# Start of a decoder layer on TensorE: inputs and the first three weight units taken in by pairs of feature tiles

## What is computed

```
h = RMSNorm(x) * norm_mix                 # x (512, 1024)
proj = h @ w_in                           # 30 column blocks of 128
ya, yb, yc = attention A, gated recurrence B, block-sparse attention C of proj
x = x + concat(ya, yb, yc) @ w_out
x = x + GatedMLP(conv3(RMSNorm(x) @ w_up)) @ w_down
x = x + sigmoid(RMSNorm(x) @ w_pg) * (p @ w_pe)
return RMSNorm(x)
```

## Time and profile before

| | us |
|---|---|
| median of three runs | 750.8 |
| lowest, highest | 748.54, 750.8 |
| profiled execution | 747.16 |
| its span on the core | 745.4 |

### The profile page before, as it was taken

The page is one execution under the profiler, slowest core; times in us unless marked ns, Lnnn a source line. Parts: engine busy times, 40 slices in busy tenths (PEclk is TensorE's granted clock), DMA queues, the critical chain, the costliest instruction groups (busy, mean ns, idle before and its releaser), DMA issues.

```text
span 745.4 us, 10529 instructions
## 1 busy us (share of the span) xinstructions
PE 723.8 (97%) x3935; PEld 592.6 (80%) x3935; DVE 453.2 (61%) x705; ACT 314.2 (42%) x545; POOL 122.4 (16%) x99
## 2 busy tenths in 40 slices
PE   5999999998999999999999999999999999999993
PEld 4778777877888878778888888888888888888883
DVE  4754779748866645576767676676763333324555
ACT  7652214255665634444333343433332223226344
POOL 1030000025655432201011101101110001000000
PEclk9999999999999999999999999999999999999998
DMA  8333221312222102333332323333215332333202
GB/s 263 113 89 112 58 58 57 118 53 85 86 86 86 58 29 85 113 107 92 97 102 85 112 84 107 90 94 103 85 49 163 98 105 79 99 113 113 86 0 114
DMA packets 121745, 69.44 MB, mean 93 GB/s; under 512 B 2658, under 2 KB 118450, under 8 KB 121706
## 3 DMA queue, kind: packets, MB, share of 16 engines
q1 hardware_dynamic: 119982, 65.72, 29.4%
q10 hardware_dynamic: 1724, 3.19, 1.3%
HBM read 66.77 MB, written 2.13 MB: 92 GB/s over the span
## 4 chain that ended last, share of the span: by engine, by line
PE 88%; DVE 5%; ACT 3%; issue 1%; DMA 1%; SPq 0%; POOL 0%; DVEq 0%; ACTq 0%
PE bank L466 26%; PE bank L468 26%; PE bank L467 26%; PE bank L506 2%; PE bank L606 2%; DVE w_lo L1161 2%; PE bank L588 2%; PE bank L574 1%; DMA raw<-in_w_in 1%; ACT w_hi L834 1%; PE bank L576 1%; DVE h_lo L1167 1%; DVE x_t L1252 1%; PE bank L540 1%; ACT scratch L852 1%
## 5 line engine op out<-in xcount | busy, mean ns | idle before, releaser
L466 PE MATMUL bank<-h_hi,w_hi 128*128 128x512 f32 (+1 forms) x664 | 264.3, 398 | 2.6 <-DVE h_lo L1167 2.6
L468 PE MATMUL bank<-h_hi,w_lo 128*128 128x512 f32 (+1 forms) x664 | 257.8, 388 | 0.0
L467 PE MATMUL bank<-h_lo,w_hi 128*128 128x512 f32 (+1 forms) x664 | 257.7, 388 | 0.0
L834 ACT ACTIVATE w_hi<-raw 128x1024 fp32r<-128x1024 f32 (+1 forms) x116 | 120.8, 1042 | 288.2 <-PE bank L468 288.1
L1161 DVE TENSOR_TENSOR w_lo<-raw,w_hi 128x1024 fp32r<-128x1024 f32 (+1 forms) x116 | 144.7, 1247 | 113.0 <-ACT w_hi L834 112.8
L466 PEld LDWEIGHTS bank<-h_hi,w_hi 128*128 128x128 f32 x664 | 125.1, 188 | 28.6 <-DVE w_lo L1161 2.8
L468 PEld LDWEIGHTS bank<-h_hi,w_lo 128*128 128x128 f32 x664 | 125.1, 188 | 26.2
L467 PEld LDWEIGHTS bank<-h_lo,w_hi 128*128 128x128 f32 x664 | 125.3, 189 | 24.2 <-issue 1.0
L1647 POOL TENSOR_SCALAR probs<-probs,row_inv 128x512 f32<-128x512 f32 (+3 forms) x48 | 66.0, 1379 | 148.4 <-DVE row_inv L1432 148.1
L466 PE MATMUL bank<-act_hi,w_hi 128*128 128x512 f32 x176 | 68.6, 389 | 0.0
L468 PE MATMUL bank<-act_hi,w_lo 128*128 128x512 f32 x176 | 68.5, 389 | 0.0
(11 more groups left out here) (186 smaller groups left out, 791.7 us busy)
## 6 DMA issues: line engine op xcount, KB each, us to landing
raw<-in_w_up SPq DMA_DIRECT2D x44, 512.0 KB, 3.6
raw<-in_w_in SPq DMA_DIRECT2D x30, 512.0 KB, 3.7
raw<-in_w_down SPq DMA_DIRECT2D x16, 512.0 KB, 3.2
raw<-in_w_out SPq DMA_DIRECT2D x8, 512.0 KB, 3.3
raw<-in_w_pg SPq DMA_DIRECT2D x8, 512.0 KB, 3.3
bias<-bias_table ACTq DMA_DIRECT2D x6, 512.0 KB, 3.7
raw<-in_w_down SPq DMA_DIRECT2D x8, 384.0 KB, 2.8
x_rows<-in_x SPq DMA_DIRECT2D x4, 512.0 KB, 5.8
```

Of the source, the lines that this page charges most:

```text
L466: pe.matmul(bank, hi, x_hi, start=first, stop=False)
L467: pe.matmul(bank, hi, x_lo, start=False, stop=False)
L468: return pe.matmul(bank, lo, x_hi, start=False, stop=last)
L834: act.activation(w_hi[:, u % SPLIT, 0:nk * ncol], raw[:, u % RAW, 0:nk * ncol], ACT.Copy)\
```

## The change

The start is cut by pairs of feature tiles instead of by token tiles.

- **Loads.** SyncE issues for each pair j of feature tiles x's 256 columns (512 KB, runs of 1 KB) and then the two row tiles of units 0, 1 and 2 (128 KB each, runs of 512 bytes). The identity goes to ScalarE's queue as its first DMA, and `norm_mix` has a semaphore of its own.
- **TensorE.** It begins with seven matmuls on a block of zeros (`q_both`, which VectorE fills first) and two more before the first product. It turns x pair by pair and runs units 0, 1 and 2 side by side in banks 0, 1 and 2. The row spread, the conv turn and the bias look-up stand two units later (in units 3, 4 and 5).
- **ScalarE and VectorE.** High and low parts of h are made straight from PSUM, in turns with the weight pieces of 256 elements, and x is copied to `x_t` one feature tile at a time. ScalarE squares all four row tiles afterwards, then splits units 3, 4 and 5. Further splits are made three units ahead up to unit 8.
- **Banks.** The groups up to 7 use banks 0 to 3 by turns, later ones banks 0 and 1.

```diff
+FIRST = 3
+PAIRS_K = KT // 2
+WIDE = 8
...
+def bank_of(group):
+
+    return group % 4 if group < WIDE else group % 2
+
+
+def frees(group):
+
+    return None if group < 4 else group - 4 if group < WIDE + 2 else group - 2
+
+
+def split_at(u):
+
+    return {1: None, 2: None, 3: 6, 4: 7, 5: 8, 6: None}.get(u, u + 2)
...
-            for t in range(TT):
-                sp.dma_start(x_rows[:, t, :], a["x"][0, t * P:(t + 1) * P, :]).then_inc(x_in[t], 16)
-                if t == 0:
-                    sp.dma_start(square[:, 0:P], a["c_square"][:, 0:P]).then_inc(ident_in, 16)
-            load_unit(0)
-            load_unit(1)
+            for j in range(PAIRS_K):
+                cols = slice(2 * j * P, (2 * j + 2) * P)
+                sp.dma_start(x_rows[:, :, cols], a["x"][0, :, cols].rearrange("(t p) c -> p t c", p=P)).then_inc(x_in[j], 16)
+                for u in range(FIRST):
+                    name, _, _, c0, ncol = UNITS[u]
+                    sp.dma_start(raw[:, u, cols].rearrange("p (k c) -> p k c", c=ncol),
+                                 w_dram[name][cols, c0:c0 + ncol].rearrange("(k p) c -> p k c", p=P)).then_inc(piece_in[u][j], 16)
             sp.dma_start(square[:, P:4 * P], a["c_square"][:, P:4 * P]).then_inc(square_in, 16)
-            load_unit(2)
...
+            def turn_x(j):
+
+                pe.wait_ge(x_in[j], 16)
+                for k in (2 * j, 2 * j + 1):
+                    if j >= 2:
+
+                        pe.wait_ge(h_lo_ready, k - 3)
+                        pe.wait_ge(x_kept_dve if k % 2 else x_kept_act, j - 1)
+                    for t in range(TT):
+                        mm = pe.transpose(banks[4 + k % 4][:, t * P:(t + 1) * P], x_rows[:, t, k * P:(k + 1) * P], ident)
+                    mm.then_inc(x_turned, 1)
...
+            pe.wait_ge(blank_ready, 1)
+            keep_warm(7)
             pe.wait_ge(ident_in, 16)
...
+            pe.wait_ge(mix_in, 16)
+            pe.transpose(banks[3][:, 0:KT], vec_rows[0:KT, :], ident[0:KT, 0:KT]).then_inc(vec_turned, 1)
+            turn_x(0)
+            keep_warm(2)
+            for j in range(PAIRS_K):
+                first_products(0, j)
+                first_products(1, j)
+                if j == 0:
+                    pe.wait_ge(vec_in, 16 * 4)
+                    pe.transpose(banks[3][:, P:P + 4 * KT + 1], vec_rows[:, :], ident[0:4 * KT + 1, 0:4 * KT + 1])\
                       .then_inc(vec_turned, 1)
+                if j < PAIRS_K - 1:
+                    turn_x(j + 1)
+                first_products(2, j)
...
-            for u in range(PROJ):
+            for u in range(FIRST, PROJ):
                 begin_unit(u, GROUP_OF[u])
...
-                    if u == 1 and k == 5:
+                    if u == 3 and k == 7:
                         pe.wait_ge(square_in, 16)
                         spread_row()
...
+            for j in range(PAIRS_K):
+                first_gain(2 * j)
+                first_split(0, j)
+                first_gain(2 * j + 1)
+                first_split(1, j)
+                first_split(2, j)
+                act.wait_ge(h_lo_ready, 2 * j + 1)
+                act.activation(x_t[:, 2 * j, :], banks[4 + 2 * j % 4][:, :], ACT.Copy).then_inc(x_kept_act, 1)
...
             for t in range(TT):
...
+                square_rows(t)
+            split_hi(3)
+            split_hi(4)
+            split_hi(5)
             act.wait_ge(filled, 1)
+            spread()
...
+            for j in range(PAIRS_K):
+                first_lo_x(2 * j)
+                first_split(0, j)
+                first_lo_x(2 * j + 1)
+                first_split(1, j)
+                first_split(2, j)
+                dve.tensor_copy(x_t[:, 2 * j + 1, :], banks[4 + (2 * j + 1) % 4][:, :]).then_inc(x_kept_dve, 1)
+            split_lo(3)
             rstd_of_rows()
             dve.wait_ge(ident_in, 16)
             diagonal()
+            split_lo(4)
+            split_lo(5)
```

More of the change, by code:

```diff
@@ L474, in begin_unit @@
                 pe.wait_ge(wlo_ready, rnd * UP_ROUND + (u + 1))
-                if group >= 2:
-                    wait_taken(pe, group - 2, rnd)
+                if frees(group) is not None:
+                    wait_taken(pe, frees(group), rnd)
             def sum_squares(stage):
@@ L638, in mixers, with keep_warm @@
                     turn_values(slot - 1)
-            pe.wait_ge(ident_in, 16)
[L642 to L655, removed]
+            def keep_warm(count):
+                for _ in range(count):
+                    pe.matmul(banks[2][:, :], q_both[:, 0, 1, 0:P], q_both[:, 0, 0, :], start=True, stop=True)
@@ new lines, in turn_x, with first_products @@
+            def turn_x(j):
[7 more added lines that the diff above has]
+                    mm.then_inc(x_turned, 1)
+            def first_products(u, j):
+                if j < PAIRS_K - 1:
+                    pe.wait_ge(first_lo, FIRST * j + u + 1)
+                else:
+                    pe.wait_ge(wlo_ready, u + 1)
+                for k in (2 * j, 2 * j + 1):
+                    if u == 0:
+                        wait_h(0, k)
+                    mm = products(banks[bank_of(u)][:, :], u, k, P, 0, h_hi[:, k, :], h_lo[:, k, :], k == 0, k == KT - 1)
+                if j == PAIRS_K - 1:
+                    mm.then_inc(unit_done, 1)
@@ L1047, in _, with first_gain, first_split @@
[L1047 to L1053, removed]
+            def first_gain(k):
+                act.wait_ge(x_turned, k + 1)
+                act.activation(h_hi[:, k, :], banks[4 + k % 4][:, :], ACT.Copy, scale=vec_cols[:, k:k + 1]).then_inc(h_hi_ready, 1)
+            def first_split(u, j):
+                cols = slice(2 * j * P, (2 * j + 2) * P)
+                act.wait_ge(piece_in[u][j], 16)
+                act.activation(w_hi[:, u, cols], raw[:, u, cols], ACT.Copy)\
+                   .then_inc(first_hi if j < PAIRS_K - 1 else whi_ready, 1)
@@ L1069, in beside_unit @@
                         split_piece(u, n)
-                if u + 2 < N_UNITS:
-                    split_hi(u + 2)
+                if split_at(u) is not None and u + 2 < N_UNITS:
+                    split_hi(split_at(u))
                 if u == PE_UNITS:
                     act.preload_act_table_set("natural_log_exp_and_others")
-                if u == 1:
-                    spread()
                 if u == PE_UNITS + 1:
@@ L1108, in beside_unit @@
                     square_result(u - 2 - PG)
-            for u in range(UP + UP_PEELED):
+            for u in range(1, UP + UP_PEELED):
                 beside_unit(u)
@@ L1221, in take @@
                 kind, i, unit = GROUPS[group]
-                bank = acc[group % 2]
+                bank = banks[bank_of(group)]
                 dve.wait_ge(unit_done, rnd * UP_ROUND + (unit + 1))
@@ L1473, in mixers, with first_lo_x, first_split @@
                         split_piece(slot, hh)
[L1476 to L1485 removed]
+            def first_lo_x(k):
+                dve.wait_ge(h_hi_ready, k + 1)
+                dve.scalar_tensor_tensor(out=h_lo[:, k, :], in0=banks[4 + k % 4][:, :], scalar=vec_cols[:, k:k + 1],
+                                         in1=h_hi[:, k, :].bitcast(F32), op0=ALU.mult, op1=ALU.subtract).then_inc(h_lo_ready, 1)
+            def first_split(u, j):
+                cols = slice(2 * j * P, (2 * j + 2) * P)
+                if j < PAIRS_K - 1:
+                    dve.wait_ge(first_hi, FIRST * j + u + 1)
+                else:
+                    dve.wait_ge(whi_ready, u + 1)
+                dve.tensor_tensor(w_lo[:, u, cols], raw[:, u, cols], w_hi[:, u, cols].bitcast(F32), ALU.subtract)\
+                   .then_inc(first_lo if j < PAIRS_K - 1 else wlo_ready, 1)
+            for j in range(PAIRS_K):
+                first_lo_x(2 * j)
[5 more added lines that the diff above has]
+            split_lo(3)
             rstd_of_rows()
```

62 lines of the change are left out of this document (30 added, 32 removed).

## The result

The changed kernel takes 750.93 us, the median of 20 runs (749.85 to 751.32); the kernel before, run beside it, 749.59 (20 runs, 748.15 to 752.43). The ratio is 1.0017 with a 95% interval of 1.0009 to 1.0025: 0.7 to 1.9 us slower, which is inside the 0.3% that was called no change. The profiled execution of the new kernel took 750.94 us (span 749.2), against 747.16 (span 745.4) of the one before.

The account below looks back on a forecast made before the run. TensorE, busy 97% of the span, bounds the kernel, losing time only by standing still or at low clock. Unit 6 0.7 us earlier plus 1.2 lost to the clock gives +0.5 on 750.8: 751.3 us, range 748.6 to 754.0.

Parts of the forecast that it names:

- The forecast case: Whole kernel: early start spent on stands before units 3 and 4 and low clock; +0.5 us, 751.3; chance 0.52.
- First product: Start of the kernel: TensorE's first product at 7.8 us, between 7.0 and 8.8, 6.9 us earlier than before.
- Rival 2: First products and behind the stand at unit 3: low clock at both places, +2.7 us, 753.5; chance 0.14.
- X: Point where x tile 6 is turned, with the three units side by side: P0 + 13.3 us.
- P0: Start of TensorE's first product, forecast at 7.8 us.
- They hide: Units 0 to 2: per pair, ScalarE's 2.7 us and VectorE's slightly longer work fit behind TensorE's 4.9 us.
- The stand before unit 3: TensorE waits 3.8 us before unit 3, whose weight split comes behind ScalarE's four row squares.
- The row spread before unit 4: Late spread in unit 3 makes TensorE wait 1.1 us for unit 0's bank before unit 4.
- The clock's share: Behind the stand at unit 3 the clock falls to half; 1.2 us lost, range 1.1 to 1.7.
- Rival 1: Clock stays high through the stand at unit 3: -0.7 to -1.5 us, 749.3 to 750.1; chance 0.22.
- rival 3: Loads at the start: small pieces load slowly, at 142 GB/s, moving X by 4.3 us; +4.8, 755.6; chance 0.05.
- The sum at unit 6: Start of unit 6, same state in both programs: 51.2 us against 51.87, -0.7 before 1.2 for the clock.

Follow-up runs that it names:

- run 4: The changed kernel without its nine warm-up matmuls on zeros at the start (the fill of the zeros stays): 752.54 us, ratio 1.0035.
- run 1: The changed kernel with 13 matmuls on zeros filling TensorE's stand before unit 3: 749.89 us, ratio 0.9994.
- run 2: The changed kernel with ScalarE's four row squares moved two by two behind pairs 1 and 2: 748.92 us, ratio 0.9992.
- run 3: As run 2, with Newton chain and diagonal ahead of VectorE's unit 3 split and the row spread earlier in unit 3: 747.51 us, ratio 0.9965.
- run 5: The changed kernel with earlier squares and spread, unit 3 loaded in pieces and split in halves, and the wait at 178 us filled: 743.81 us, ratio 0.9923.
- run 6: The changed kernel with nine overwritten matmuls filling the wait at 178 us: 749.70 us, ratio 1.0002.
- run 7: The kernel before with nine overwritten matmuls filling the wait at 178 us: 748.62 us, ratio 0.9994.

## Why the prediction was right, and where its terms were off

The forecast case came about: one stand ahead of unit 3 for ScalarE's squares, a clock fall behind it, a second short stand for the first bank, and a time within 0.3% of before. Taken term by term on the profiled execution:

- **First product**: 7.8 forecast, 8.04 measured (+0.2). The warm-ups did keep the clock up: eight transposes in 1.09 us, products 0.23 apart. Rival 2 (low clock at both places) is out, and run 4 shows what it would have cost.
- **The three units up to x tile 6 turned (X)**: P0 + 13.3 forecast, 14.5 measured (the turn of the last pair begins at 21.98, and ScalarE's gain on its first half starts at 22.61, so X is about 22.55), and this is the largest miss (+1.2). The transposes took what was counted. The matmuls did not: the 48 were put at 0.227 each, 10.9 us, but take 12.1 (to 11.00, 12.02 to 16.60, 17.39 to 21.98). About 0.6 of the 1.2 is that behind each interruption the second matmul starts 0.1 late; the row the price came from, was of one stretch without interruptions. The other half is a wait that the prediction put at nothing. Between the third unit's block and the next pair's first product stand 0.23 to 0.25 us (13.27 to 13.73, 18.62 to 19.10, less one matmul), and the row of the weight load names what ends it:

```profile
18.63 0.42 DVE L1561 TENSOR_TENSOR w_lo<-raw,w_hi 128x256 fp32r<-128x256 f32 x1
19.10 0.19 PEld L486 LDWEIGHTS bank<-h_hi,w_hi 128*128 128x128 f32 x1 [0.52 <-DVE w_lo L1561]
```

  It is VectorE's low part of the weight piece, which ends 0.05 before (19.05). The prediction had the numbers: the low parts come 2.0 after the first tile of a pair is turned, and TensorE has 0.4 of transposes and 1.36 of the third unit's block to fill them, 1.76. It used them for the last pair and wrote "They hide" for the two before. The same wait stands at the same places in the profiles of runs 1 to 6; no run takes it away.
- **The stand before unit 3**: 3.8 forecast, 3.3 measured. ScalarE was as forecast: squares 1.18 apart (1.19). The prediction said that the load of unit 3 "is not the last", which is true, but without the squares the stand is only 1.0 us shorter (run 2). Moving the squares therefore brings 1.0 us of the stand and not 3.8.
- **The row spread before unit 4**: 1.1 forecast, 0.93 measured; unit 4 starts 9.15 after unit 3, which is 7.41 without the clock's share, against 7.4.
- **The clock's share**: 1.2 forecast (1.1 to 1.7), 1.74 measured, 1.6 by run 1. It fell at the end of the stand (at 32.5), the case for which the prediction had 1.7. The prediction took a value near the low end, and no row spoke for that. Rival 1 (the clock stays up) was wrong for this stand of 3.3 us in the profiled execution, though it is what runs 2 and 3 show behind 2.3 and 2.1.
- **Loads**: rival 3 is out. The 128 KB pieces, with the last loads of x between them, came at 367 GB/s (8 to 12 us), and in the list of waits no load of x or of a piece holds TensorE. The Trainium skill (DMA: Bandwidth & Descriptors, Bandwidth), whose advice of 1 MiB or more pointed to this rival, isn't borne out by this row for pieces queued one behind another.
- **The sum at unit 6**: 51.2 + 1.2 = 52.4 forecast, 54.24 measured, 1.84 late: +0.2 (first product), +1.2 (X), -0.3 (unit 3 starts 9.6 after X and not 9.9), +0.5 (clock), +0.2 between units 4 and 6.

So the change at unit 6 was forecast at +0.5 and is +2.4 in the trace. In the medians it is +1.3 (0.7 to 1.9), and 1.1 between runs 6 and 7. One reason is that the medians of before hold executions with a slower start than its profiled one, as run 7's. How much of the 1.1 between 2.4 and 1.3 this is, no run measures; it stays open. The number itself, 751.3 against 750.93, is nearer than the terms deserve: it was laid on a median of three runs (750.8) that fell into the upper group; on 749.59 the same +0.5 would have given 750.1, 0.8 too low. The mechanism was right: the lead is spent in front of units 3 and 4 and on the clock. But the forecast sum without the clock was -0.7, and it came out at +0.6, so the sign rested on the 1.2 for which no row spoke, and it held because X was longer too. The last microsecond was right by luck: the base was 1.2 too high and the change, by the medians, 0.8 too small.

## What to carry to other kernels

An early start is worth only what the next shared resource passes on: follow it up to the point where both programs are in the same state, and for each wait on the way name the one that ends second to last too, because removing the last one only hands the wait over (3.3 to 2.3 us here, until the load was also cut up). The stand of 3.3 us here cost its length and then half of the next matmuls' pace, 1.6 us; where such a stand can't be removed, matmuls that compute nothing can give the second part back. A wait worked out for one round of a loop holds for the other rounds as well, until a row says otherwise. And before a time is forecast from a median of three, look whether the times fall into groups.

## What the runs showed of the hardware that was not expected

- **The same stand, with and without a fall.** Behind stands of 3.2 to 3.3 us (the changed kernel, runs 4 and 6) the clock fell to 0.50 for 3 to 7 us in each profile; behind 2.3 and 2.1 us (runs 2 and 3) it stayed at 1.00 at that place, though behind 2.6 and 2.8 us (before, run 7) it fell. Behind the 2.0 us wait at 178 us it fell in the profiles of the changed kernel and run 2 and not in those of before and of runs 1, 3 and 4.
- **Half pace at a granted clock of 1.00.** Without warm-ups the first 12 products are 0.43 us apart while the stretch says 1.00; it shows the low rate only by the distance of the matmuls:

```profile
9.00:10.00 1.00, 1.00 (x4) 0.81 (x3) 0.85 (x2) 0.00 (x0) 0.00 (x0) 1.00 1.12 357
10.00:11.00 1.00, 1.00 (x4) 0.81 (x3) 0.00 (x0) 0.00 (x0) 0.00 (x0) 1.00 1.12 365
```

  The seven warm-ups of the changed kernel run at the same pace (3.35 us for seven), and the transposes behind them at nearly twice that of run 4's (1.09 against 1.97 for eight).
- **Every interruption cost TensorE 0.1 us more than its length.** The first product behind transposes or behind a wait is followed by the next after 0.31 to 0.34 us and not 0.23 (12.02 to 12.34, 17.39 to 17.71). A change of bank within products costs nothing (9.31, 9.54, 9.77, where unit 0's block gives way to unit 1's). What the 0.1 is isn't shown.
